# A three-block network at float32 accuracy on one core: the scaling of each head's probabilities moves from GpSimd to VectorE

## The chip, the cores and the metric

The kernel runs on one core of a Trainium2 chip. The metric is the device time of one execution in microseconds (us). The core has five engines that run their own instruction streams and meet at semaphores: TensorE (PE in the profile, with PEld for its weight loads), VectorE (DVE), ScalarE (ACT), GpSimd (POOL) and SyncE (SP), which here issues the weight loads from memory.

## The reference

An input of 256 rows by 1024 features goes through a stack of layers. In short, and cut to what matters here:

```
h = x
h = h + moba_nsa_mixer(rmsnorm(h));  h = h + relu(rmsnorm(h) @ w1)**2 @ w2      # "even" mixer, then an MLP
h = h + fox_mixer(rmsnorm(h));       h = h + relu(rmsnorm(h) @ w1)**2 @ w2      # "fox" mixer, then an MLP
h = rmsnorm(h)
h = h + 0.5 * gate1 * swiglu(n1)                                                # gated MLP
h = h + gate2 * hybrid_mixer(n2)                                                # "dil" mixer
h = h + 0.5 * gate3 * swiglu(n3);  return rmsnorm(h)
# in each mixer, for each head, with 256 queries and 256 keys of 64 features:
s = q @ k.T * scale + bias;  s = where(mask, s, -inf)
p = exp(s - max(s)) / sum(exp(s - max(s)))         # softmax over the keys
o = gate * (p @ v)                                 # gate: a sigmoid per row, only in the NSA branches
```

The even mixer has 24 such heads: 16 NSA heads (8 heads in two branches, "selected" and "window", each with a gate per query row) and 8 MoBA heads without a gate. The fox mixer has 16 heads, the dil mixer 8, all without a gate. A ninth NSA branch over 15 compressed keys is computed beside the heads.

## The kernel before

**Weights.** 512 KB halves of the weights stream through a ring of four units. ScalarE rounds each half (`w_hi`, L737), VectorE computes the rest (`w_lo`, L1141), and TensorE multiplies with three products (high by low, low by high, high by high), which gives float32 accuracy. Each unit counts in `unit_used` when TensorE is done, and SyncE then loads the unit that takes its place.

**Mixers.** A mixer is a list of ticks, a tick being a half or a quarter of a weight unit of a projection. `plan` at the top of the file fixes, before the kernel is built, which heads' scores, turns and products lie in which tick; all engines walk through the same list. In a tick TensorE does, in this order: the scores of a head (`scores`, L1872 and L1873, into one PSUM bank, `BANK_S`), the turning (transposition) of the probabilities of an earlier head (`turn_probs`, L1881), for two heads at a time the products with the values (`products`, L1899), the extras of the mixer, and then its part of the projection (L1662 to L1664).

**One head.** After the scores VectorE adds the bias and finds the row minimum of the negated logits (L1352, `logit` and `low`, once for query rows 128 to 255 with 256 keys, once for query rows 0 to 127 with 128 keys). ScalarE takes the exponential into `prob` (L908), with the row sums in `den`, and counts `probs_ready`. VectorE takes the reciprocals of the two sums (L1371, `wgt`, 128 x 2). GpSimd multiplies `prob` in place by the reciprocal and by the gate (`scale`, L599), a column of 128 x 1 each, or by the constant 1.0 where the head has no gate, and counts `probs_scaled`. TensorE waits for that in `turn_probs`, some two ticks later. There are four `prob` buffers, two `logit` buffers, but only one scores bank: TensorE may write the scores of head i only when VectorE has finished the logits of head i-1:

```
if i >= 1:
    pe.wait_ge(logits_ready, i)
```

**VectorE's tick**, in program order: the logits of the tick's head, the split of a finished projection (`stack`, L1333, two instructions, after the last tick of a unit), the copy of a turned odd head (L1364, `probT`), one half of `w_lo` where one is due, the reciprocals (L1371), the extras, and the split of finished output tiles (L1377). The extras in the even mixer are the steps of the compressed branch (L1549 to L1551, L1561 to L1564, L1569 to L1574). Instructions on an engine start in program order, so what stands behind a long one waits for it. The helper `chain(ins)` makes VectorE wait until `ins` has been completed.

**GpSimd's stream** between the scalings: it sets zeros, issues small loads, and in the fox mixer `mask(c)` adds the causal triangle to the gates of four heads at a time (L607, L608), each of which VectorE waits for before the first logits of those four heads.

Of the kernel before, what the change touches and what calls it, by code (L numbers as in the profile page):

```python
# [22 lines left out]
ALU = mybir.AluOpType  # L23
# [60 lines left out]
EVEN, FOX, DIL = (0, 24), (24, 40), (40, 48)  # L84
# [102 lines left out]
def build(nc, stream, ada, cols, x, c_row, rel_table, rel_pick, dil_bias, pool_mat, b_forget, final_norm, g_final, out):  # L187
    ctx = ExitStack()
    with ctx:
        base = [-(-nc.sbuf_base // 64) * 64]  # L190

        def place(name, shape, dt=F32, at=None):
            size = -(-int(np.prod(shape[1:])) * 4 // 64) * 64
            if at is None:
                at = base[0]
                base[0] += size
            return nc.alloc_sbuf_tensor_at(name, list(shape), dt, offset=at)

        def sem(name):
            return ctx.enter_context(nc.semaphore(name))  # L200
# [50 lines left out]
        prob = place("prob", [P, 4, SW])  # L251
# [21 lines left out]
        den = place("den", [P, CMP_COL + 16])  # L273
        wgt = place("wgt", [P, CMP_COL + 16])
        gates = place("gates", [P, TT, 24])
# [100 lines left out]
        weight_ready = sem("weight_ready")  # L376
        probs_scaled = sem("probs_scaled")
# [46 lines left out]
        heads = []  # L424
# [10 lines left out]
        for hh in range(HEADS):  # L435
# [3 lines left out]

        TILES = {"even": [(4, 0, 0), (5, 0, T), (6, 1, 0), (7, 1, T)] + [(m, m % 2, 0) for m in range(4)],  # L440
                 "fox": [(m, m % 2, 0) for m in range(8)], "dil": [(m, m % 2, 0) for m in range(4)]}
        TILES_BEFORE = {"even": 0, "fox": 8, "dil": 16}

        def out_col(i):
# [141 lines left out]
        def _(pool):  # L586
# [3 lines left out]
                pool.memset(k_lo2[0:HD, tiles, 1, :].bitcast(F32), 0.0).then_inc(zeros_ready, 1)  # L590
                pool.wait_ge(zeros_ready, before + 2)

            def scale(first, last):
                for i in range(first, last):
                    pool.wait_ge(weight_ready, i + 1)
                    for t, lo, hi in ((1, 0, 256), (0, 256, 384)):
                        p_ = prob[:, i % 4, lo:hi]
                        gate = 1.0 if heads[i][5] is None else gates[:, t, heads[i][5]:heads[i][5] + 1]
                        ins = pool.tensor_scalar(p_, p_, wgt[:, 2 * i + t:2 * i + t + 1], gate, ALU.mult, ALU.mult)  # L599
                    ins.then_inc(probs_scaled, 1)  # L600

            def mask(c):

                pool.wait_ge(cum_landed[c], 16)
                four = slice(4 * c, 4 * c + 4)
                tri = pc_("tri", P).unsqueeze(1).to_broadcast([P, 4, P])
                pool.tensor_tensor(cum_early[:, four, :], cum_row[:, four, 0:P], tri, ALU.add).then_inc(masked, 1)  # L607
                pool.tensor_tensor(cum_row[:, four, P:T], cum_row[:, four, P:T], tri, ALU.add).then_inc(masked, 1)  # L608
# [18 lines left out]
            def store_gate(j):  # L627
                pool.wait_ge(gain_ready, j + 1)
                pool.dma_start(bass.AP(gate_dram, j * D, [[KT, P], [1, KT]]), gatec[:, KT * j:KT * j + KT]).then_inc(gate_stored, 16)
# [18 lines left out]
            pool.dma_start(rel_band[:, HEADS:16, :], bass.AP(rel_dram, HEADS * (REL + 1), [[1, P], [REL + 1, HEADS], [1, T]])).then_inc(rel_landed[0], 16)  # L648
            pool.wait_ge(unit_used, FIRST["kskw"])
            pool.dma_start(rel_band[:, 0:HEADS, :], bass.AP(rel_dram, 0, [[1, P], [REL + 1, HEADS], [1, T]])).then_inc(rel_landed[1], 16)  # L650
            scale(*EVEN)

            pool.wait_ge(bank_turned, TURN["mlp0"] + 8)
            zeros(slice(6, 8), 2)
# [10 lines left out]
            def forget_gates(c):  # L665
                if c > 0:
                    pool.wait_ge(unit_used, FIRST["qk_fox"] + c - 1)
                pool.dma_start(cum_row[:, 4 * c:4 * c + 4, :], bass.AP(cum_dram, 4 * c * T, [[0, P], [T, 4], [1, T]])).then_inc(cum_landed[c], 16)
# [4 lines left out]
            mask(1)  # L673
            forget_gates(2)
            forget_gates(3)
            scale(FOX[0], FOX[0] + 2)
            mask(2)
            scale(FOX[0] + 2, FOX[0] + 6)
            mask(3)
            scale(FOX[0] + 6, FOX[1])  # L680

            pool.wait_ge(bank_turned, TURN["mlp1"] + 8)
            pool.wait_ge(unit_used, FIRST["mlp1"] + 3)
# [19 lines left out]
            pool.wait_ge(bank_turned, TURN["gmix"] + 8)  # L703
            gate_rows(1)
            store_gate(2)
            scale(*DIL)

            round_half("gf2")
            pool.wait_ge(bank_turned, TURN["gf2"] + 8)
# [415 lines left out]
        def _(dve):  # L1125
            steps = [0]

            def chain(ins):
                steps[0] += 1
                ins.then_inc(dve_step, 1)  # L1130
                dve.wait_ge(dve_step, steps[0])
# [3 lines left out]
            def rest_half():  # L1135

                if halves[0] < 2 * N_UNITS:
                    u, part = halves[0] // 2, halves[0] % 2
                    dve.wait_ge(hi_ready, halves[0] + 1)
                    part_ = slice(HALF * part, HALF * part + HALF)  # L1140
                    nc.vector.tensor_tensor(w_lo[:, u % RING, part_], raw[:, u % RING, part_], w_hi[:, u % RING, part_].bitcast(F32),  # L1141
                                            ALU.subtract).then_inc(lo_ready, 1)
                    halves[0] += 1
# [181 lines left out]
            def stack(key, halves_=(0, 1)):  # L1325
                bank, keys, tile = STACKS[key]
                for b in halves_:
                    dve.wait_ge(feat_hi, 2 * STACK_NO[key] + b + 1)
                    rows_ = slice(HD * b, HD * b + HD)
                    src = ps[bank][rows_, :].rearrange("p (a b) -> p a b", a=2)  # L1330
                    hi = (k_two if keys else q_two)[rows_, tile:tile + 2, b, :]
                    dst = k_lo2[rows_, tile:tile + 2, b, :] if keys else q_two[HD * (1 - b):HD * (1 - b) + HD, tile:tile + 2, b, :]
                    ins = nc.vector.scalar_tensor_tensor(out=dst, in0=src, scalar=1.0 if keys else -0.125, in1=hi.bitcast(F32),  # L1333
                                                         op0=ALU.mult, op1=ALU.subtract)
                    ins.then_inc(feat_taken, 1)
# [6 lines left out]
            def mixer(kind, ticks, extras):  # L1342
                prev = None
                for tick in ticks:
                    for i in tick.s:
                        bias = heads[i][4]
                        dve.wait_ge(scores_done, i + 1)
                        if i >= 2:
                            dve.wait_ge(probs_ready, i - 1)
                        for t, lo, hi in ((1, 0, 256), (0, 256, 384)):  # L1350
                            kk = 2 * i + t
                            ins = nc.vector.tensor_tensor_reduce(  # L1352
                                logit[:, i % 2, lo:hi], ps[BANK_S][:, lo:hi], bias(t),
                                1.0, 4 * BIG, ALU.add, ALU.min, low[:, kk:kk + 1])
                        ins.then_inc(logits_ready, 1)
                    stacks = prev is not None and prev.part == prev.parts - 1 and (prev.tag, prev.j) in STACKS
                    if stacks:
                        stack((prev.tag, prev.j), (0,))
                    for j in tick.t:
                        if j % 2:  # L1360
                            dve.wait_ge(probsT_done, j + 1)
                            if j >= TURNED:
                                dve.wait_ge(pv_done, (j - TURNED) // 2 + 1)
                            nc.vector.tensor_copy(probT[:, j % TURNED, :], ps[BANK_PT][:, 0:SW]).then_inc(probsT_dve, 1)  # L1364
                    if stacks:
                        stack((prev.tag, prev.j), (1,))
                    if halves[0] < tick.halves:
                        rest_half()
                    for i in tick.s:
                        dve.wait_ge(probs_ready, i + 1)  # L1370
                        nc.vector.reciprocal(wgt[:, 2 * i:2 * i + 2], den[:, 2 * i:2 * i + 2]).then_inc(weight_ready, 1)  # L1371
                    extras(tick)
                    if prev is not None:
                        for n in prev.closed:
                            m, bank, c0 = TILES[kind][n]
                            dve.wait_ge(tile_hi, TILES_BEFORE[kind] + (n | 1 if kind == "even" and n < 4 else n) + 1)
                            nc.vector.tensor_tensor(q_two[:, m, 1, :], ps[bank][:, c0:c0 + T], q_two[:, m, 0, :].bitcast(F32),  # L1377
                                                    ALU.subtract).then_inc(tile_split, 1)
                    prev = tick
# [280 lines left out]
        def _(pe):  # L1660
# [223 lines left out]
            def products(kind, i):  # L1884
# [5 lines left out]
                if i >= NSA:  # L1890
# [3 lines left out]
                    elif n >= 2:  # L1894
                        pe.wait_ge(tile_split, TILES_BEFORE[kind] + n - 1)
                for block, lo, hi in ((0, 0, T), (1, T, SW)):
# [8 lines left out]
            def out_part(kind, j, part, parts=4):  # L1905
# [4 lines left out]
                elif part == 0:  # L1910
                    pe.wait_ge(tile_split, TILES_BEFORE[kind] + 2 * ((j - 2 if kind == "dil" else j) + 1))
                if part == 0 and j == 0:
# [380 lines left out]
```

## Time and profile before

| | |
|---|---|
| median of 3 runs | 1077.68 us (1077.62 to 1077.70) |
| the profiled execution | 1077.94 us, of which the traced span is 1075.8 us |
| busy, share of the span | PE 99%, DVE 74%, ACT 62%, POOL 11% |
| granted TensorE clock | 0.999 of full speed |

How to read it: the span is the time from the first to the last instruction of the trace; the profiled execution took 2.1 us more than its span. A busy share is an average over stages. PE is counted as busy when matmuls overlap one another, so a short hold of TensorE can hide in longer intervals between matmuls.

### The profile page before, as it was taken

Reading aid. Unit: us, or ns where it says so; the run is one execution under the profiler, and the core shown is the slowest. Engines: PE = TensorE matmul, PEld = TensorE weight load, DVE = VectorE, ACT = ScalarE, POOL = GpSimd, SP = SyncE. Lnnn points to the kernel's source line nnn. Section 1 sums busy time; section 2 is a strip of 40 time slices with the busy share of each in tenths; the row PEclk is TensorE's granted clock in tenths of the full one; section 3 lists DMA queues with packets and bytes.
Section 4 is the critical chain, followed back from the end, with each engine's and each line's share of the span. In section 5 each row is a group of like instructions: output and inputs, shape, how many; then the busy total and the mean of one; then the engine's idle time right before and its main releaser. Section 6 shows DMA issues by size and latency. Waiting matters only on the chain.

```text
span 1075.8 us, 16103 instructions
## 1 busy us (share of the span) xinstructions
PE 1065.0 (99%) x6102; PEld 915.4 (85%) x6102; DVE 792.8 (74%) x1384; ACT 669.7 (62%) x1186; POOL 119.1 (11%) x212
## 2 busy tenths in 40 slices
PE   9999999999999999999999999999999999999997
PEld 7998788888888997888888888888878978888885
DVE  7767677787877776787767788987885778566575
ACT  7678677565666776766556765454476767445443
POOL 1033110010100531020000000111000210000000
PEclk9999999999999999999999999999999999999999
DMA  9932359888865633687877568878745445565551
GB/s 360 326 127 86 111 176 341 290 300 301 305 217 170 229 127 111 214 322 264 282 244 272 181 213 296 294 265 319 275 164 187 139 155 181 193 196 195 182 191 59
DMA packets 65533, 238.33 MB, mean 222 GB/s; under 512 B 7429, under 2 KB 8613, under 8 KB 64688
## 3 DMA queue, kind: packets, MB, share of 16 engines
q1 hardware_dynamic: 51696, 188.82, 51.8%
q0 software_dynamic: 13040, 47.85, 11.9%
q8 instruction: 49, 0.80, 0.3%
q10 hardware_dynamic: 720, 0.62, 0.2%
q14 instruction: 28, 0.23, 0.1%
HBM read 236.15 MB, written 1.11 MB: 221 GB/s over the span
## 4 chain that ended last, share of the span: by engine, by line
PE 93%; DVE 4%; ACT 1%; issue 1%; DMA 0%; POOL 0%; DVEq 0%; ACTq 0%
PE bank L1693 23%; PE bank L1662 15%; PE bank L1663 15%; PE bank L1664 15%; PE bank L1697 12%; PE bank L1830 2%; PE bank L1899 1%; PE bank L1881 1%; PE bank L1720 1%; PE bank L1715 1%; PE bank L1723 1%; PE bank L1768 1%; PE bank L1873 1%; PE bank L1872 1%; DVE w_lo L1141 1%
## 5 line engine op out<-in xcount | busy, mean ns | idle before, releaser
L1141 DVE TENSOR_TENSOR w_lo<-raw,w_hi 128x1024 fp32r<-128x1024 f32 x348 | 414.2, 1229 | 68.3 <-ACT w_hi L737 65.8
L737 ACT ACTIVATE w_hi<-raw 128x1024 fp32r<-128x1024 f32 x345 | 348.8, 1052 | 64.4 <-DMA raw<-in_stream 64.1
L1693 PE MATMUL bank<-a_two,w_hi 128*128 128x512 f32 x1088 | 271.9, 392 | 0.0
L1693 PEld LDWEIGHTS bank<-a_two,w_hi 128*128 128x128 f32 x1088 | 198.4, 188 | 37.4
L946 ACT ACTIVATE cross<-bank 128x256 f32<-128x256 f32 x136 | 51.4, 381 | 190.7 <-PE bank L1697 190.5
L1662 PE MATMUL bank<-w_lo,hid_hi 128*128 128x512 f32 x432 | 169.2, 392 | 0.2
L1663 PE MATMUL bank<-w_hi,hid_lo 128*128 128x512 f32 x432 | 168.7, 390 | 0.0
L1664 PE MATMUL bank<-w_hi,hid_hi 128*128 128x512 f32 x432 | 168.1, 389 | 0.0
L1697 PEld LDWEIGHTS bank<-a_two,w_lo 128*128 128x128 f32 x1088 | 148.4, 190 | 10.6
L1697 PE MATMUL bank<-a_two,w_lo 128*128 128x256 f32 x1088 | 151.7, 282 | 0.0
L1385 DVE TENSOR_TENSOR hid_act<-bank,cross 128x256 f32<-128x256 f32 x96 | 39.6, 422 | 86.7 <-ACT cross L946 86.5
L1664 PEld LDWEIGHTS bank<-w_hi,hid_hi 128*128 128x128 f32 x432 | 81.1, 188 | 17.2
L1662 PEld LDWEIGHTS bank<-w_lo,hid_hi 128*128 128x128 f32 x432 | 81.3, 188 | 16.5 <-DVE hid_lo L1392 1.0
L1663 PEld LDWEIGHTS bank<-w_hi,hid_lo 128*128 128x128 f32 x432 | 81.3, 188 | 14.9
L1662 PE MATMUL bank<-a_two,w_hi 128*128 128x256 f32 x320 | 93.5, 292 | 0.0
L1664 PE MATMUL bank<-a_two,w_hi 128*128 128x256 f32 x320 | 90.4, 283 | 0.0
L1663 PE MATMUL bank<-a_two,w_lo 128*128 128x256 f32 x320 | 90.4, 282 | 0.0
L1419 DVE CUSTOM_DVE_ANT_0 ada_raw<-ada_raw,silu_row 128x1024 f32<-128x1024 f32 x72 | 84.8, 1219 | 4.3 <-DMA ada_raw<-in_ada 2.3
L614 POOL DMA_DIRECT2D ada_raw<-in_ada x72 | 38.1, 530 | 322.5 <-DVE modc L1419 322.5
L1662 PEld LDWEIGHTS bank<-a_two,w_hi 128*128 128x128 f32 x320 | 61.1, 191 | 2.4 <-issue 2.1
L1663 PEld LDWEIGHTS bank<-a_two,w_lo 128*128 128x128 f32 x320 | 61.2, 191 | 0.1
L1664 PEld LDWEIGHTS bank<-a_two,w_hi 128*128 128x128 f32 x320 | 61.1, 191 | 0.0
(234 smaller groups left out, 1339.9 us busy)
## 6 DMA issues: line engine op xcount, KB each, us to landing
raw<-in_stream SPq DMA_DIRECT2D x348, 512.0 KB, 5.0
ada_raw<-in_ada POOLq DMA_DIRECT2D x72, 512.0 KB, 5.3
cmpw<-in_stream SPq DMA_DIRECT2D x4, 1024.0 KB, 9.6
rel_band<-rel_scratch POOLq DMA_DIRECT2D x2, 1024.0 KB, 11.2
cum_row<-cum_scratch POOLq DMA_DIRECT2D x4, 512.0 KB, 5.7
gate_row<-gate_scratch POOLq DMA_DIRECT2D x3, 512.0 KB, 6.3
h<-in_x SPq DMA_DIRECT2D x2, 512.0 KB, 4.4
silu_row<-in_c_row POOLq DMA_DIRECT2D x2, 512.0 KB, 6.4
```

Source lines behind the costliest of these rows:

```text
L614: pool.dma_start(ada_raw[:, p % ADA_BUFS, :], ada[p]).then_inc(ada_landed[p % ADA_BUFS], 16)
L737: nc.scalar.activation(w_hi[:, u % RING, part_], raw[:, u % RING, part_], ACT.Copy).then_inc(hi_ready, 1)
L946: nc.scalar.activation(cross[:, slot, nt, :], ps[bank][:, T:2 * T], ACT.Copy).then_inc(done, 1)
L1141: nc.vector.tensor_tensor(w_lo[:, u % RING, part_], raw[:, u % RING, part_], w_hi[:, u % RING, part_].bitcast(F32), ALU.subtract).then_inc ...
L1385: nc.vector.tensor_tensor(to[:, nt * T:(nt + 1) * T], ps[bank][:, 0:T], cross[:, slot, nt, :], ALU.add).then_inc(done, 1)
L1419: nc.vector.tensor_tensor_reduce(part, part, silu_row[:, :], 1.0, 0.0, ALU.mult, ALU.add, modc[:, p:p + 1]).then_inc(ada_done, 1)
L1662: nc.tensor.matmul(dst, l_hi, r_lo, start=start, stop=False)
L1663: nc.tensor.matmul(dst, l_lo, r_hi, start=False, stop=False)
L1664: return nc.tensor.matmul(dst, l_hi, r_hi, start=False, stop=stop)
L1693: nc.tensor.matmul(ps[bank][:, 0:2 * T], wh[:, k, cols_], a_two[:, :, k, :], start=k == 0, stop=False)
L1697: ins = nc.tensor.matmul(ps[bank][:, T:2 * T], wl[:, k, cols_], a_hi[:, k, :], start=False, stop=k == KT - 1)
L1830: ins = nc.tensor.matmul(ps[BANK_A[2 * t + n]][:, 0:w], rows_[:, 2 * j + k, ts], weights[:, k, 512 * n:512 * n + w], start=(j, k, term) == ...
```

## The change

The 96 GpSimd instructions that scale the probabilities (2 for each of 48 heads) are removed, with their function. VectorE issues the same two multiplications itself, in place, behind the reciprocals of the head, and counts `probs_scaled`. Between the reciprocals and the first multiplication VectorE waits for the reciprocals' completion (`chain`). `weight_ready` is no longer counted, since all three mixers are in `SCALED_BY_DVE`. GpSimd's masks of heads 8 to 15 of the fox mixer stand directly behind its loads.

```
+        SCALED_BY_DVE = ("even", "fox", "dil")
...
-            def scale(first, last):
-                for i in range(first, last):
-                    pool.wait_ge(weight_ready, i + 1)
-                    for t, lo, hi in ((1, 0, 256), (0, 256, 384)):
-                        p_ = prob[:, i % 4, lo:hi]
-                        gate = 1.0 if heads[i][5] is None else gates[:, t, heads[i][5]:heads[i][5] + 1]
-                        ins = pool.tensor_scalar(p_, p_, wgt[:, 2 * i + t:2 * i + t + 1], gate, ALU.mult, ALU.mult)
-                    ins.then_inc(probs_scaled, 1)
...
-            scale(*EVEN)
...
-            scale(FOX[0], FOX[0] + 2)
             mask(2)
-            scale(FOX[0] + 2, FOX[0] + 6)
             mask(3)
-            scale(FOX[0] + 6, FOX[1])
...
-            scale(*DIL)
...
                     for i in tick.s:
                         dve.wait_ge(probs_ready, i + 1)
-                        nc.vector.reciprocal(wgt[:, 2 * i:2 * i + 2], den[:, 2 * i:2 * i + 2]).then_inc(weight_ready, 1)
+                        weights_ = nc.vector.reciprocal(wgt[:, 2 * i:2 * i + 2], den[:, 2 * i:2 * i + 2])
+                        if kind not in SCALED_BY_DVE:
+                            weights_.then_inc(weight_ready, 1)
+                            continue
+                        chain(weights_)
+                        for t, lo, hi in ((1, 0, 256), (0, 256, 384)):
+                            p_ = prob[:, i % 4, lo:hi]
+                            gate = 1.0 if heads[i][5] is None else gates[:, t, heads[i][5]:heads[i][5] + 1]
+                            ins = nc.vector.tensor_scalar(p_, p_, wgt[:, 2 * i + t:2 * i + t + 1], gate, ALU.mult, ALU.mult)
+                        ins.then_inc(probs_scaled, 1)
```

On VectorE, in the even mixer, this is the stretch of heads 11 to 13 of the kernel before: the reciprocals of head 11, the logits of head 12, a copy, a weight half, the reciprocals of head 12 and the compressed branch ahead of the logits of head 13.

```order
L1371 RECIPROCAL wgt<-den 128x2
L1352 ISA logit,low<-bank,rel_band 128x256
L1352 ISA low 128x1
L1352 ISA logit,low<-bank,rel_band 128x128
L1352 ISA low 128x1
L1364 COPY probT<-bank 128x384
L1141 TENSOR_TENSOR w_lo<-raw,w_hi 128x1024
L1371 RECIPROCAL wgt<-den 128x2
L1569 TENSOR_REDUCE den<-pc 128x16
```

The same stretch on VectorE with the change (line numbers there are those of the changed file: L1358 is the reciprocal, L1339 the logits, L1366 the new multiplication, L1128 the weight half):

```order
L1358 RECIPROCAL wgt<-den 128x2
L1366 TENSOR_SCALAR prob<-prob,wgt,gates 128x256
L1366 TENSOR_SCALAR prob<-prob,wgt,gates 128x128
L1339 ISA logit,low<-bank,rel_band 128x256
L1339 ISA low 128x1
L1339 ISA logit,low<-bank,rel_band 128x128
L1339 ISA low 128x1
L1351 COPY probT<-bank 128x384
L1128 TENSOR_TENSOR w_lo<-raw,w_hi 128x1024
L1358 RECIPROCAL wgt<-den 128x2
L1366 TENSOR_SCALAR prob<-prob,wgt,gates 128x256
L1366 TENSOR_SCALAR prob<-prob,wgt,gates 128x128
```

Each head's two multiplications now stand between its reciprocals and the logits of the next head.

On GpSimd, in the fox mixer, the scalings of the kernel before stand between the third load (issued twice in a row for heads 8 to 11 and 12 to 15) and the mask of heads 8 to 11:

```order
L668 DMA cum_row<-cum_scratch 128x1024 x2
L599 TENSOR_SCALAR prob<-prob,wgt 128x256
L599 TENSOR_SCALAR prob<-prob,wgt 128x128
L599 TENSOR_SCALAR prob<-prob,wgt 128x256
L599 TENSOR_SCALAR prob<-prob,wgt 128x128
L607 TENSOR_TENSOR cum_early<-cum_row,par 128x512
L608 TENSOR_TENSOR cum_row<-cum_row,par 128x4x128
L599 TENSOR_SCALAR prob<-prob,wgt 128x256
```

The same place on GpSimd with the change (L659 is the load, L599 and L600 the mask):

```order
L659 DMA cum_row<-cum_scratch 128x1024 x2
L599 TENSOR_TENSOR cum_early<-cum_row,par 128x512
L600 TENSOR_TENSOR cum_row<-cum_row,par 128x4x128
L599 TENSOR_TENSOR cum_early<-cum_row,par 128x512
L600 TENSOR_TENSOR cum_row<-cum_row,par 128x4x128
L609 DMA silu_row<-in_c_row 128x1024
```

The two masks follow the loads directly, and GpSimd then waits for the MLP.

## Rows read from the trace of the kernel before

**Rows 1.** The page: busy time of each engine, and the chain's shares.

```profile
PE 1065.0 (99%) x6102; PEld 915.4 (85%) x6102; DVE 792.8 (74%) x1384; ACT 669.7 (62%) x1186; POOL 119.1 (11%) x212
...
PE 93%; DVE 4%; ACT 1%; issue 1%; DMA 0%; POOL 0%; DVEq 0%; ACTq 0%
```

**Rows 2.** The stretch 76 to 92 us: busy time and number of instructions.

```profile
76.00:92.00 16.00, 15.73 (x140) 14.60 (x139) 12.76 (x49) 11.79 (x33) 5.61 (x12) 1.00 0.20 67
```

**Rows 3.** The chain that ended last, in the even mixer: start, us, what.

```profile
78.72 0.17 DVE wgt L1371
```

**Rows 4.** TensorE's timeline: start of the scores of heads 11 to 14.

```profile
80.75 0.28 PE L1872 MATMUL bank<-k_two,q_two 128*128 128x256 f32 x1
...
84.59 0.28 PE L1872 MATMUL bank<-k_two,q_two 128*128 128x256 f32 x1
...
86.78 0.28 PE L1872 MATMUL bank<-k_two,q_two 128*128 128x256 f32 x1
...
90.16 0.35 PE L1872 MATMUL bank<-k_two,q_two 128*128 128x256 f32 x1 [0.27 <-DVE low L1352]
```

**Rows 5.** VectorE's timeline: heads 11 to 14, and head 18.

```profile
81.91 0.16 DVE L1371 RECIPROCAL wgt<-den 128x2 f32<-128x2 f32 x1
...
83.61 0.42 DVE L1352 CUSTOM_DVE_ANT_0 logit<-bank,rel_band 128x256 f32<-128x256 f32 x1
...
85.60 0.17 DVE L1371 RECIPROCAL wgt<-den 128x2 f32<-128x2 f32 x1
85.80 0.42 DVE L1352 CUSTOM_DVE_ANT_0 logit<-bank,rel_band 128x256 f32<-128x256 f32 x1
...
87.96 0.15 DVE L1371 RECIPROCAL wgt<-den 128x2 f32<-128x2 f32 x1
...
89.39 0.41 DVE L1352 CUSTOM_DVE_ANT_0 logit<-bank,rel_band 128x256 f32<-128x256 f32 x1
...
91.07 0.17 DVE L1371 RECIPROCAL wgt<-den 128x2 f32<-128x2 f32 x1 [1.05 <-ACT prob L908]
...
104.16 0.42 DVE L1352 CUSTOM_DVE_ANT_0 logit<-bank,rel_band 128x256 f32<-128x256 f32 x1 [1.93 <-PE bank L1873]
```

**Rows 6.** TensorE's timeline: the scores of head 18.

```profile
103.54 0.28 PE L1872 MATMUL bank<-k_two,q_two 128*128 128x256 f32 x1
```

**Rows 7.** GpSimd's scalings: count, duration min/median/max in ns, starts.

```profile
L599 POOL TENSOR_SCALAR prob<-prob,wgt x64: 364/479/1423, 100.2 to 865.5; 128x256 f32<-128x256 f32 x32, 128x128 f32<-128x128 f32 x32
L599 POOL TENSOR_SCALAR prob<-prob,wgt,gates x32: 436/502/561, 53.1 to 98.0; 128x256 f32<-128x256 f32 x16, 128x128 f32<-128x128 f32 x16
```

**Rows 8.** VectorE's groups by form: busy us, mean ns of one.

```profile
L1189 DVE TENSOR_SCALAR tok<-h,stat 128x512 f32<-128x512 f32 x11 | 5.2, 485 | 0.3
...
L1176 DVE TENSOR_SCALAR stat<-stat 128x1 f32<-128x1 f32 x14 | 3.0, 214 | 4.8 <-ACT tok L753 4.4
...
L1167 DVE TENSOR_SCALAR stat<-stat 128x1 f32<-128x1 f32 x14 | 2.0, 146 | 0.1
...
L1648 DVE SCALAR_TENSOR_TENSOR tok<-h,stat,row 128x256 f32<-128x256 f32 x4 | 1.8, 481 | 0.1
```

**Rows 9.** VectorE's timeline: a scaling of 512 columns and its successor.

```profile
609.25 0.49 DVE L1189 TENSOR_SCALAR tok<-h,fin 128x512 f32<-128x512 f32 x1
609.66 1.22 DVE L1141 TENSOR_TENSOR w_lo<-raw,w_hi 128x1024 fp32r<-128x1024 f32 x1
```

**Rows 10.** TensorE's timeline: scores of heads 11 and 12 of the fox mixer.

```profile
401.39 0.28 PE L1872 MATMUL bank<-k_two,q_two 128*128 128x256 f32 x1
...
403.54 0.36 PE L1872 MATMUL bank<-k_two,q_two 128*128 128x256 f32 x1
```

**Rows 11.** VectorE's timeline: a weight half in the fox mixer.

```profile
358.37 2.07 DVE L1141 TENSOR_TENSOR w_lo<-raw,w_hi 128x1024 fp32r<-128x1024 f32 x1 [0.30 <-ACT w_hi L737]
```

**Rows 12.** The chain in the dil mixer.

```profile
854.00 0.69 DVE q_two L1333
...
854.98 1.88 POOL prob L599 x2
```

## The prediction

> **What bounds the kernel now.** I read the page first, then the busy time by stretch, then the chain that ended last, then the timelines of single engines. TensorE is busy for 99% of the span, and the chain runs through it for 93%, but 4% of it, some 43 us, lie on VectorE [rows 1]. So the question is where TensorE is held by VectorE, and how close VectorE is to holding it elsewhere. In the middle of the even mixer the chain leaves TensorE for more than 11 us: it stands on VectorE at 78.72 with the reciprocals of a head, and comes back with the scores of head 14 at 90.16 [rows 3, 4]. In the 16 us around it VectorE is busy for 12.76 and ScalarE for 11.79 [rows 2]. TensorE shows only one hold there, 0.27 us ahead of those scores [rows 4]. So this stretch is balanced: TensorE and VectorE both run almost without slack, and the link is the single scores bank.
>
> Three intervals describe the link. From the start of the scores to the start of the logits, 0.62 us (103.54 and 104.16, where VectorE had been waiting) [rows 5, 6]. From the start of the logits to the earliest start of the next scores, 0.77 us (89.39 and 90.16) [rows 4, 5]. From the start of the logits to the start of the reciprocals when only the exponential lies between, 1.68 us (89.39 and 91.07) [rows 5]; I use 1.70. I call these starts S, L and R.
>
> **What is removed.** 96 GpSimd instructions with medians of 0.48 and 0.50 us [rows 7]. Nothing but the turns of TensorE waits for them, two ticks later, and POOL has no measurable share of the chain [rows 1]. One place shows: in the dil mixer a pair took 1.88 us and the chain goes through it [rows 12]. I value what comes back there at 0.2 us.
>
> **What is added.** Two VectorE multiplications for each head. The trace has no such instruction of 256 or 128 columns, but it has the same operation at other sizes: 146 ns with one column and two constants, 214 ns with one column and one operand per partition, 485 ns with 512 columns [rows 8]. A per-partition operand thus adds 68 ns and a column (485 - 214) / 512 = 0.53 ns. That gives 350 and 282 ns without a gate, 418 and 350 ns with one. An instruction's successor starts some 0.075 us before its end (609.25 to 609.66 for 0.485) [rows 9], but not across a wait for completion: head 11's reciprocals take 0.17 and the logits start 0.20 behind them [rows 5]. So in place of one interval of 0.20 there are 0.20, then 0.34, then 0.38: s = 0.71 us with a gate and, the same way, 0.58 without. Over 16 gated and 32 other heads this is 29.9 us more on VectorE, and the sum depends on how much of it TensorE's ticks absorb.
>
> The Trainium skill (VectorE: DVE Perf Modes, the section on the TRN2 errata) gives 58 cycles plus columns over the mode's factor for such an instruction; at 0.96 GHz and factor 2 that is an estimate of 0.33 us for 512 columns, where this trace has 0.485. By the page, s would be 0.44 us or less and the sum below about 4 us. The measured row decides here.
>
> **The even mixer, worked.** Each head obeys: S is the tick's place in TensorE's stream plus the delay p so far, or the previous L + 0.77, whichever is later, and in the second case p grows by the difference. L is S + 0.62, or the time when VectorE is free. R is L + 1.70, or L + 0.65 plus what stands between (1.60 for a copy and a weight half, 1.40 for a split projection, about 1.1 for a weight half alone). VectorE is then free at R + 0.10 + s plus its extras. With s = 0 this recurrence gives back the trace to about 0.1 us, with a hold of 0.4 where the trace has 0.27, and 0.1 more at the end. With s = 0.71 it reaches head 10 with p = 1.12 (grown at heads 2, 3 and 6, where a weight half or a split stands in the tick) and L = 81.59. From there, with the starts of before from [rows 4, 5]:
>
> Head 10 has R = 81.59 + 0.65 + 1.60 = 83.84; with 0.81 and the compressed branch's 1.62 (81.91 to 83.61 less the usual interval) head 11 has L = 86.27. Its scores would start at 80.75 + 1.12 = 81.87 but wait for 81.59 + 0.77 = 82.36: p = 1.61. Head 12's would start at 84.59 + 1.61 = 86.20 and wait for 87.04: p = 2.45. Head 11 has R = 88.32, so head 12 has L = 89.13; head 13's scores go from 89.23 to 89.90: p = 3.12. Head 12 has R = 91.38, and with 0.81 and 1.33 of the branch (87.96 to 89.39) head 13 has L = 93.52; head 14's scores, unheld at 89.89 + 3.12 = 93.01, wait for 94.29: p = 4.40. Behind it ticks with products and longer parts absorb the additions (before head 18 VectorE had waited 1.93 us [rows 5]), until heads 22 and 23 add 0.7 and 0.2: p = 5.26. The same recurrence without the additions has 0.52, so the term is **+4.7 us**.
>
> **The fox mixer.** Its ticks hold half a weight unit, not a quarter, and by the recurrence the additions of 0.58 are absorbed up to head 11. From there the ticks are the quarters of the output projection, 2.15 us (401.39 to 403.54) [rows 10]: the logits of heads 12 and 13 come 0.7 and 1.5 later, and two holds of 0.5 and 0.9 follow. The term is +1.3, less what s = 0 gives in the same recurrence (0.2): +1.2 us.
>
> **The dil mixer.** The same pattern at heads 4 to 6, and the split that ends at 854.69, for which TensorE waits already [rows 12], now begins 0.7 later, since the logits in front of it are late. Holds of 0.7, 0.1 and 0.5, less 0.2 for the pair that took 1.88: +1.2 us.
>
> Sum: 4.7 + 1.2 + 1.2 = 7.1 us. The profiled execution took 1077.94 us (span 1075.8); with 7.1 that is 1085.0. The median of the runs is 0.26 lower, so I forecast 1085.0 for the median, rounded up by that much. TensorE has hardly any wait behind the mixers in which a delay could be given back, so it stays to the end.
>
> **What hides the rest.** Of 29.9 us some 23 cost nothing, because VectorE stood waiting for scores (1.93 before head 18) or for the exponential. If the exponential moves with the late logits, that second cover is gone; the recurrence has this in it.
>
> **The masks.** GpSimd's masks of heads 8 to 15 now run back to back near 369 us. A weight half on VectorE, which takes 1.22 elsewhere [rows 9], took 2.07 beside an earlier mask [rows 11], 0.85 more. At worst two of VectorE's instructions are held so, in the long ticks that absorb the additions. I take nothing, with an upper end of 1.5 us. The Trainium skill (SBUF — State Buffer, section Who interferes with whom) has a rule for this: a GpSimd instruction and a VectorE instruction in a two-port mode or with two SBUF inputs exclude each other for their whole length. The 2.07 agrees with it, as does the pair of 1.88.
>
> **Bounds.** For s from below: the shortest form of the operation, 146 ns, and nothing for the wait for completion, would be near 0.3 for both; nearer to the 512-column row is 0.45, at which the recurrence gives 2.4, 0.8 and 0.4, so 3.6 us in all. From above: at the rate of the 256-column row that reads two tiles, 481 ns [rows 8], the first multiplication costs 0.13 more and the second 0.07, and with another 0.05 for the second operand s is 0.95, which gives 7.6, 1.6 and 2.0, with the masks 12 us. The operation itself is nearest to the 485 ns row, so I take 0.71.
>
> **Rivals.** (a) *Dearer multiplications*, s near 0.9, with or without the masks: +9.5 to +12, about 1088.5. For it: in-place operands and short tiles that no row shows. Against: three rows of the same operation lie on one line. 0.15. (b) *Cheaper, better hidden*, s near 0.5 or a TensorE stream with more give than the recurrence allows, as its 0.4 for 0.27 hints: +2.5 to +4.5, about 1081.5. 0.17. (c) *Absorbed: not slower.* The scores of the next head are late only if VectorE's backlog exceeds the slack of the tick; if TensorE's short matmuls were themselves running behind their weight loads, a hold of up to 0.7 at each score would be made up in the same tick, and the seven holds would vanish. The dil turn then comes 0.2 earlier: 1077.5. It decides if TensorE can make up more than 0.7 us per tick. Against: TensorE is busy for 15.73 of the 16 us [rows 2] and has no idle time to give. 0.08. (d) *The masks as a new wait*: they take VectorE in ticks without slack, 1 to 2 us more, 1086.5, inside my range; it counts with the forecast.
>
> **The numbers.** The forecast, +5 to +9 us, has 0.60, (a) 0.15, (b) 0.17, (c) 0.08. The range 1081.0 to 1089.5 takes in both bounds of s save the very ends. A measurement of this kernel tells about 0.2%, 2.2 us, from no change. (c) and the lowest part of (b) give same 0.08; faster, which no mechanism here gives, 0.03; slower 0.89.
>
> **What would show it.** In the profile after: the new VectorE group at 0.42 and 0.35 us with a gate, 0.35 and 0.28 without; TensorE's scores (L1872 before) waiting for VectorE's logits at heads 11 to 14 with a total near 3.5 us, and a chain with several us more on VectorE between 50 and 120 us; the even mixer longer by 4.7, the fox and dil mixers by about 1.2 each; the MLPs unchanged. Wrong would be the whole if the scores of head 14 start before 92, or if the multiplications differ by more than 0.1 us from these durations.

## The result and the profile after

The changed kernel takes 1084.63 us (median of 6 runs, 1084.08 to 1085.26), the kernel before 1077.64 (1077.59 to 1077.70): 1.0064 times as long, 95% interval [1.0053, 1.0075], 7.0 us slower. The profiled execution took 1084.26 us, its span is 1082.5.

The page, to be read against [rows 1]:

```profile
span 1082.5 us, 16103 instructions
...
PE 1067.5 (99%) x6102; PEld 915.1 (85%) x6102; DVE 819.7 (76%) x1480; ACT 670.1 (62%) x1186; POOL 70.4 (7%) x116
...
PE 89%; DVE 7%; ACT 2%; issue 1%; DMA 0%; POOL 0%; DVEq 0%; ACTq 0%; POOLq 0%
```

VectorE is busy for 26.9 us more, with 96 instructions more, GpSimd for 48.7 us less. Of the chain VectorE has 7% in place of 4%, some 30 us more, and TensorE 89% in place of 93%. That is more than the 7.0 us by which the kernel is longer: the chain also turns to VectorE in stretches through which it ran on TensorE before.

The new groups of VectorE by form (count, then busy us and mean ns), against the estimates from [rows 8]:

```profile
L1366 DVE TENSOR_SCALAR prob<-prob,wgt 128x256 f32<-128x256 f32 x32 | 12.0, 374 | 1.1
...
L1366 DVE TENSOR_SCALAR prob<-prob,wgt 128x128 f32<-128x128 f32 x32 | 9.8, 307 | 0.0
...
L1366 DVE TENSOR_SCALAR prob<-prob,wgt,gates 128x256 f32<-128x256 f32 x16 | 6.6, 412 | 0.6
L1366 DVE TENSOR_SCALAR prob<-prob,wgt,gates 128x128 f32<-128x128 f32 x16 | 5.5, 342 | 0.0
```

412 and 342 ns stand against the estimated 418 and 350. Without a gate the means are above the estimated 350 and 282, because of one pair beside GpSimd's masks; the shortest of the 128-column ones took 279, and the medians are 353 and 281.

What TensorE's matmuls waited for (us in total, times, longest us):

```profile
PE bank L1868 <- DVE low L1339: 4.3, 9, 1.0
...
PE bank L1868 <- DVE q_two L1320: 0.2, 1, 0.2
```

The scores (L1868 here) waited nine times for VectorE's logits; before it was one wait of 0.27 us [rows 4]. TensorE's timeline at heads 11 to 14 of the even mixer (start, us, and in brackets the idle time ahead):

```profile
81.96 0.36 PE L1868 MATMUL bank<-k_two,q_two 128*128 128x256 f32 x1 [0.30 <-DVE low L1339]
...
86.53 0.36 PE L1868 MATMUL bank<-k_two,q_two 128*128 128x256 f32 x1 [0.51 <-DVE low L1339]
...
89.43 0.36 PE L1868 MATMUL bank<-k_two,q_two 128*128 128x256 f32 x1 [0.48 <-DVE low L1339]
...
93.62 0.36 PE L1868 MATMUL bank<-k_two,q_two 128*128 128x256 f32 x1 [1.01 <-DVE low L1339]
```

Against [rows 4] these starts are later by 1.21, 1.94, 2.65 and 3.46 us. Head 0's is 0.40 earlier (49.99 against 50.39), which has nothing to do with the scaling: no head has been scaled by then. So the scaling holds TensorE back by 1.61, 2.34, 3.05 and 3.86; the recurrence had 1.61, 2.45, 3.12 and 4.40, the last less 0.27 for the hold that was there before. (The idle times in brackets, 2.3 us in all, are less than the 2.7 us by which the delay grows at these four heads, since a part of each hold hides in longer intervals between matmuls.)

This reading, the start of a head's scores less the start of the same head's in the kernel before, is the measure of all that follows. The table gives by how much it grew from the first to the last head of each mixer, in us (from the timelines of each run's trace):

```
                              even    fox     dil    median of runs   before beside it
changed kernel                4.6     2.0     0.3       1084.63          1077.64
e1 VectorE: even alone        4.6      0       0        1082.11          1077.70
e2 VectorE: fox alone          0      2.1      0        1079.55          1077.70
e3 VectorE: dil alone          0       0      0.3       1077.79          1077.70
e4 masks held back            4.6     1.2     0.3       1083.52          1077.70
e5 scaled twice              13.8     5.5     2.2       1100.37          1077.83
e6 behind next logits         2.6     1.9     0.2       1082.73          1077.83
e7 e6 + masks held back       2.6     1.2     0.2       1081.85          1077.83
e8 e7, behind the split too   2.0     1.35    0.8       1081.96          1077.71
e9 128 columns only           2.25    0.45   -0.3       1079.77          1077.71
```

The last column is the kernel before, run again beside each group of experiments. Each version has one trace.

### The profile page after: what moved, and what is told of

Read it like the earlier page. It is cut to its first block, busy times and chain, and to the rows that moved or that the text cites. A ratio compares the mean times of both kernels' runs of the same rounds, so it can differ in the third digit from the quotient of the medians.

```text
span 1082.5 us, 16103 instructions
## 1 busy us (share of the span) xinstructions
PE 1067.5 (99%) x6102; PEld 915.1 (85%) x6102; DVE 819.7 (76%) x1480; ACT 670.1 (62%) x1186; POOL 70.4 (7%) x116
## 4 chain that ended last, share of the span: by engine, by line
PE 89%; DVE 7%; ACT 2%; issue 1%; DMA 0%; POOL 0%; DVEq 0%; ACTq 0%; POOLq 0%
PE bank L1689 23%; PE bank L1658 14%; PE bank L1659 14%; PE bank L1660 14%; PE bank L1693 12%; PE bank L1826 2%; PE bank L1895 1%; DVE w_lo L1128 1%; PE bank L1716 1%; PE bank L1711 1%; PE bank L1719 1%; PE bank L1877 1%; PE bank L1764 1%; DVE logit L1339 1%; PE bank L1868 1%
## 5 line engine op out<-in xcount | busy, mean ns | idle before, releaser
L1128 DVE TENSOR_TENSOR w_lo<-raw,w_hi 128x1024 fp32r<-128x1024 f32 x348 | 414.1, 1229 | 65.3 <-ACT w_hi L724 62.5
L895 ACT ACTIVATE prob<-logit,low 128x256 f32<-128x256 f32 x96 | 42.9, 447 | 36.5 <-DVE low L1339 36.2
```

The source lines that it names most:

```text
L895: ins = nc.scalar.activation(prob[:, i % 4, lo:hi], logit[:, i % 2, lo:hi], ACT.Exp, scale=-1.0, bias=low[:, kk:kk + 1], accum_out=den[:, ...
```

## The experiments

**Each mixer alone (e1, e2, e3).** The scaling by GpSimd is put back for the mixers that `SCALED_BY_DVE` doesn't name:

```
-        SCALED_BY_DVE = ("even", "fox", "dil")
+        SCALED_BY_DVE = ("even",)          # e1;  ("fox",) in e2;  ("dil",) in e3
```

> VectorE scales in the even mixer alone; GpSimd scales in the fox and dil mixers as before. Theory (the delay is the sum of the holds at the scores bank, mixer by mixer): TensorE ends the even mixer 4.2 us later in the trace of the changed kernel (head 23's scores at 121.25 against 117.07), and nothing gives it back, so +4.2 us, 1081.9; by the recurrence of the prediction +4.7, 1082.4. Rival (a general cost of 29.9 us more work on VectorE, shared out by heads): 15.4 of the 29.9 us of scaling are in the even mixer by number and length, so 16*0.71 + 8*0.58 = 16.0 of 29.9, +3.7 us.

> VectorE scales in the fox mixer alone. Theory: the fox mixer adds 2.0 us in the trace of the changed kernel, 0.94 at head 3, beside the masks, and 1.0 at heads 13 to 15, so 1079.6. In this kernel the masks of heads 8 to 15 run back to back too. The prediction had +1.2, 1078.9. Rival (shared out by heads): 9.3 of 29.9 us, +2.2 us; the two are not told apart by this run alone.

> VectorE scales in the dil mixer alone. Theory: +0.3 us, 1078.0, as the spacing of the scores in the trace of the changed kernel says. The prediction had +1.2, 1078.9. Rival (shared out by heads): 4.6 of 29.9 us, +1.1 us.

Measured against the kernel before: e1 1.0041 [1.0027, 1.0056], +4.4 us; e2 1.0019 [1.0009, 1.0028], +1.85 us; e3 1.0001 [0.9992, 1.0010], +0.1 us, which is no difference. The three add up to 6.4 of the 7.0 us; in the traces they grow by what they grow in the changed kernel, mixer by mixer. The delay is a sum of separate holds. A cost shared out by heads would have had 3.7 us in the even mixer, 2.2 in the fox and 1.1 in the dil mixer. The intervals of e1 and e2 hold these values too, and 1.1 us lies at the edge of the interval of e3; against it speaks the dil mixer's 0.3 in the traces, and what decides is e5, e6 and e9 below.

**The masks (e4).**

```
+            pool.wait_ge(probs_scaled, FOX[0] + 2)
             mask(2)
+            pool.wait_ge(probs_scaled, FOX[0] + 6)
             mask(3)
```

The two masks wait for the scaling of heads 1 and 5, behind which they stood before.

> The changed kernel, but GpSimd waits for the scaling of heads 1 and 5 of the fox mixer before it makes the third and the fourth mask, so that these stand where they stood before. Theory (the hold of 0.78 us at head 3 comes from the masks of heads 8 to 15 running back to back at 369 to 374 us and blocking VectorE's scaling pair of 2.04 us): that pair falls to 0.55 us and the kernel is 0.9 us faster than the changed one, 1083.7. Rival (the hold comes from the additional work alone, and the masks would only hold something else): within 0.2 us of the changed kernel, 1084.6.

Measured: 1083.52 us, 1.0055 [1.0038, 1.0072] against before; over before it has 5.8 us where the changed kernel has 7.0. The intervals of the two overlap, though no run of e4 (1083.37 to 1083.69) is as long as the shortest of the changed kernel (1084.08); the traces decide. VectorE's timeline in the changed kernel:

```profile
369.97 1.34 DVE L1128 TENSOR_TENSOR w_lo<-raw,w_hi 128x1024 fp32r<-128x1024 f32 x1 [0.26 <-ACT w_hi L724]
...
371.43 2.04 DVE L1366 TENSOR_SCALAR prob<-prob,wgt 128x256 f32<-128x256 f32 x2
373.49 0.42 DVE L1339 CUSTOM_DVE_ANT_0 logit<-bank,cum_row 128x256 f32<-128x256 f32 x1
...
376.09 0.42 DVE L1339 CUSTOM_DVE_ANT_0 logit<-bank,cum_row 128x256 f32<-128x256 f32 x1
```

and GpSimd's at the same time:

```profile
370.20 2.07 POOL L600 TENSOR_TENSOR cum_row<-cum_row,par 128x512 f32<-128x512 f32 x1
372.24 1.14 POOL L599 TENSOR_TENSOR cum_early<-cum_row,par 128x512 f32<-128x512 f32 x1
```

The pair takes 2.04 us in place of 0.55, and the mask addition that began at 370.20 takes 2.07 in place of 1.08. Read with their ends, these are two meetings in a row. The addition had begun beside the weight half (369.97 to 371.31), and from the end of that half it lasted another 0.96 us. The pair's first multiplication, begun at 371.43, took 1.00 us and ended 0.15 behind that addition, at 372.42; the second took 1.12, beside the next addition (372.24 to 373.38). In each case the one that began later ended behind the other, by its own usual length or less. The scores of head 3, at 374.28, then waited 0.78 us for the logits of head 2, and the fox mixer fell behind by 0.94 there. With the masks held back this hold is gone and the fox mixer grows by 1.2 us, not 2.0. A pair still meets a mask in e4 (1.19 us at 374.37), but the delay grows by no more than 0.2 us behind it. The Trainium skill (SBUF — State Buffer, section Who interferes with whom) says that a GpSimd instruction and a VectorE instruction in a two-port mode exclude each other for their whole length; the pair, which gets on only when the addition ahead of it ends, agrees.

**Twice the scaling (e5).** The additional results go into a buffer that is free by then, and nothing reads them (shortened, with `...` for the indices of `wgt`):

```
+                            nc.vector.tensor_scalar(logit[:, i % 2, lo:hi], p_, wgt[...], gate, ALU.mult, ALU.mult)
                             ins = nc.vector.tensor_scalar(p_, p_, wgt[...], gate, ALU.mult, ALU.mult)
```

> The changed kernel, with each scaling done twice on VectorE: an additional multiplication of the same form writes into the logits buffer, which is free by then. Adds 0.61 us per gated and 0.49 us per other head, 25.4 us of work on VectorE. Theory (slack once used up, every further us goes to TensorE; recurrence with 1.32 and 1.07 us per head): the even mixer +15.0 over the kernel before, fox +3.0, dil +2.7, so 14 us over the changed kernel, 1098.5. Rival (a fixed share, 7.0 us for 29.9 us of work, holds on): +6 us over the changed kernel, 1090.6.

Measured: 1100.37 us, 1.0209 [1.0192, 1.0226], +22.5 us over before and 15.7 over the changed kernel: some 25 us of work cost 15.7, where the first 30 had cost 7.0. The fixed share is refuted. The even mixer has 13.8 where the recurrence had 15.0, dil 2.2 for 2.7, but fox 5.5 for 3.0. There the masks hold VectorE (0.99 and 1.18 us for multiplications of 0.35 at 381.84 and 382.75), TensorE stands for 1.84 us, and then this is seen, in TensorE's timeline and in the busy time by stretch (the column before the last two is the granted clock):

```profile
382.91 0.28 PE L1660 MATMUL bank<-a_two,w_lo 128*128 128x256 f32 x1
383.03 0.28 PE L1661 MATMUL bank<-a_two,w_hi 128*128 128x256 f32 x1
385.15 0.36 PE L1869 MATMUL bank<-k_two,q_two 128*128 128x256 f32 x1 [1.84 <-DVE low L1339]
...
386.89 0.41 PE L1661 MATMUL bank<-a_two,w_hi 128*128 128x256 f32 x1
387.11 0.41 PE L1659 MATMUL bank<-a_two,w_hi 128*128 128x256 f32 x1
```

```profile
383.00:386.00 3.00, 1.16 (x8) 0.99 (x7) 2.97 (x8) 0.96 (x5) 0.78 (x1) 0.90 0.52 162
386.00:389.00 3.00, 3.00 (x17) 3.00 (x16) 2.90 (x12) 2.95 (x9) 0.00 (x0) 0.53 0.49 191
389.00:392.00 3.00, 3.00 (x28) 3.00 (x28) 2.90 (x8) 1.52 (x3) 0.00 (x0) 1.00 0.02 5
```

Behind the idle 1.84 us the matmuls follow at 0.21 us in place of 0.12, at a clock of 0.53, nearly all of it at the 1.2 GHz level, until about 389. The tick took 5.22 us (385.15 to 390.37) instead of 3.63: 1.6 us more, behind a hold of 1.84. Not every such hold does this: three others of e5, of 1.56, 1.59 and 1.55 us in the even mixer (scores of heads 11, 14 and 22), left the clock at 1.00, so these traces don't give the idle time at which it falls. No hold in the mixers of the changed kernel was longer than 1.01 us, and its clock stood at 1.00 there.

**The same work off the path (e6, e7).** VectorE scales head i only after the logits of head i+1:

```
                         ins.then_inc(logits_ready, 1)
+                    settle()                    # here in short: wait for the reciprocals, the two multiplications, probs_scaled
                     stacks = prev is not None and prev.part == prev.parts - 1 ...
```

> The changed kernel, but VectorE scales head i only behind the logits of head i+1, in the time in which it would otherwise wait for the exponential; the completion wait behind the reciprocals is then met already. Same instructions, same work. Theory (what costs is the time between the reciprocals and the next logits, since the scores bank waits for these): holds shrink, by the recurrence to 2.8 - 0.5 in the even mixer, 1.0 in fox and 0.4 in dil, so +3.7 us over the kernel before, 1081.3. Rival (VectorE's total work in the mixer decides): no change against the changed kernel, 1084.6. Second rival: the turns wait for the later scaling, and it is slower than the changed one, 1086 or more.

> The kernel of e6_late with the masks held back as in e4_masks_late. Theory: the masks cost 0.9 us here too if the additional work meets them in the same tick, so 0.9 faster than e6_late, 1080.4; but if the later place of the scaling takes VectorE out of the masks' way, no difference. Rival (work decides): 0.9 us faster than the changed kernel only, 1083.7.

Measured: e6 1.0045 [1.0030, 1.0060], +4.9 us (expected +3.7); e7 1.0036 [1.0023, 1.0050], +4.0 us, 0.9 less than e6 as expected. The even mixer falls from 4.6 to 2.6 with the same instructions, so their place matters and not only their number: the rival that total work decides, which wanted no change, is refuted. But 2.0 us of the even mixer remain at heads 12 to 14 and 22, and the fox mixer gains nothing. What TensorE waited for in e7:

```profile
PE bank L1890 <- DVE probT L1368: 0.9, 3, 0.4
PE bank L1881 <- DVE low L1355: 0.9, 3, 0.3
PE bank L1881 <- DVE q_two L1323: 0.7, 3, 0.3
```

The wait for the logits is down from 4.3 us to 0.9, but two others have grown in its place: the split of the projection (`q_two`, 0.2 us in the changed kernel) and the copy of turned probabilities (`probT`, none listed for the turns there) now stand behind the scaling.

**Behind those too (e8).** `settle()` stands after the split and the copy, ahead of the weight half; masks held back as in e4.

> The kernel of e7_late_masks_late, but the scaling of the previous head stands behind the split of the projection and the copy of turned probabilities, ahead of the weight half. Theory (in e7 the scaling delays, besides the logits, the split and the copy, and TensorE waits for these at heads 4 and 12 of the even mixer, and at heads 12 to 15 of the fox mixer): the holds on q_two and probT go, the holds on the logits stay; even +2.1, fox +0.6, dil +0.2 over the kernel before, 1080.5, that is 1.3 faster than e7. Rival (what remains is VectorE's total work): the same as e7, 1081.8. Second rival (the turn comes too late now): slower than e7.

Measured: 1.0039 [1.0024, 1.0054], +4.25 us, the same as e7 and not 1.3 faster. In the even mixer it went as expected (2.0), in the fox and dil mixers the second rival came true:

```profile
407.35 0.55 PE L1890 MATMUL bank<-par,prob 128*128 128x128 f32 x3 [1.22 <-DVE prob L1342]
```

The turn waits 1.22 us for the scaling, and another one 1.21 in the dil mixer: the multiplications now stand behind the second half of the split, at 406.75, while TensorE comes to the turn directly behind the scores of 405.48. Each of the three places tried in VectorE's tick had TensorE waiting for something.

**Only 128 columns (e9).** GpSimd scales the 256 columns, VectorE the 128, counted in a semaphore of their own, `early_scaled`, which the turn waits for as well (VectorE's part, shortened):

```
+                        weights_.then_inc(weight_ready, 1)
+                        dve.wait_ge(weight_ready, i + 1)
+                        nc.vector.tensor_scalar(prob[:, i % 4, 256:384], ..., wgt[:, 2 * i:2 * i + 1], gate, ...).then_inc(early_scaled, 1)
```

> VectorE scales the 128 columns of each head only, directly behind its reciprocals; GpSimd scales the 256 columns as before. Adds 0.38 us per gated and 0.31 us per other head on the path from the reciprocals to the next logits, 16 us in all. Theory (holds grow faster than the addition; recurrence with 0.38 and 0.31): even 2.4 - 0.5 = +1.9, fox 0.9 - 0.2 = +0.7, dil +0.2, together +2.7 over the kernel before, 1080.4. Rival (a fixed share of the work, 7.0 for 29.9 us): 16 us give +3.7, 1081.4. Second rival (the completion wait and the order cost, not the length): near the changed kernel, 1083 or more.

Measured: 1.0019 [1.0009, 1.0028], +2.1 us; expected +2.7, fixed share +3.7, which is outside the interval. The second rival, that the completion wait and the order cost and not the length, wanted 1083 or more and is refuted as well: both are there in e9. The even mixer grows by 2.25 (+1.9 expected), fox by 0.45 (+0.7), and dil shrinks by 0.3: GpSimd's pair that took 1.88 us [rows 12] no longer keeps the turn of head 3 waiting (that turn began 0.37 us behind the matmul ahead of it, and begins 0.11 behind it in e9). With e9, the changed kernel and e5, 0.38, 0.71 and 1.32 us per gated head (0.31, 0.58 and 1.07 without a gate) cost 2.25, 4.6 and 13.8 us in the even mixer. By these prices its 24 heads add 8.6, 16.0 and 29.7 us on VectorE, and of each further us 0.26 reach TensorE at first, then 0.32, and at last 0.67: cheap while slack is there, and dearer the less is left.

No version is faster than the kernel before. For the scaling GpSimd is the better of the two engines tried, since its queue is the one for which hardly anybody waits. Whether ScalarE, busy for 62%, could do it was not tried.

## Why the prediction was right

**The bound.** Right: TensorE and VectorE were balanced in the even mixer, and the single scores bank ties them. From head 11 on the holds came at the heads that the recurrence named, with the delay within 0.1 us of it up to head 13 and 0.3 at head 14. Ahead of that only the sum was right: the recurrence had 1.12 us from heads 2, 3 and 6, the trace has 1.15 from heads 3, 4 and 5 (0.58, 0.47 and 0.09), of which the one at head 4 is a wait for the split and not for the logits.

**The price of a head.** Right for the instructions, 412 and 342 ns with a gate for 418 and 350, and medians of 353 and 281 without for 350 and 282. The time from a head's reciprocals to the next logits, 0.20 us where they follow directly, was 0.79 behind heads 0 to 2 and 0.90 behind heads 3 and 11, so 0.59 to 0.70 more for s = 0.71; without a gate it was 0.66 or 0.77 for 0.19, so 0.47 to 0.58 more for 0.58. The s of the sum is the upper end of both. The Trainium skill's row (VectorE: DVE Perf Modes, the section on the TRN2 errata) had given an estimate of 0.33 us for 512 columns, and with it below about 4 us in all; [rows 8] has 0.485, and the kernel lost 7.0.

**The even mixer.** Forecast +4.7, measured 4.6 in the trace and 4.4 by e1. That is close partly by luck, as the places of the early holds and the upper end for s show.

**The fox mixer.** Forecast +1.2, measured 2.0. The step that failed is "I take nothing" for the masks: they cost 0.8 us in the traces (2.0 less the 1.2 of e4) and 1.1 to 1.2 by the medians, mostly as one hold of 0.78 at head 3. The holds at the output ticks, 0.4 and 0.5 at heads 13 and 14, came where expected and smaller than the forecast 0.5 and 0.9.

**The dil mixer.** The term was mis-sized: forecast +1.2, measured 0.3, and no difference by e3. The statement that the split "begins 0.7 later" was wrong. The scores of head 3 started at 857.83 and its logits at 858.72, 0.89 us behind, so only 0.27 later than the usual 0.62, and the split moved with them. Head 2's logits had been 0.57 later against its scores than before. Of that, 0.18 went between them and the reciprocals (1.70 us apart, 1.88 before, when they were not bound by the weight half alone), and 0.12 more behind those, where the addition took the 0.61 us that VectorE had waited for the scores of head 3. Instead of the forecast 0.7, 0.1 and 0.5 at heads 4 to 6, less 0.2 for GpSimd's pair, the delay grew by 0.15 and 0.18 and then fell by 0.09. The two errors, 0.8 too little for fox and 0.9 too much for dil, nearly cancel; the forecast of 1085.0 owes its closeness to the result to that luck as well. (Two roundings are in it as well: the addends for dil give 1.1 and not 1.2, and the median as worked out is 1084.8.)

**The rivals.** Absorption (c) is refuted in the even mixer: TensorE made up nothing of a hold in the same tick, and the delays stand unchanged through ticks with slack (3.86 at heads 14 to 21). Dearer (a) multiplications fail by the measured durations. So do cheaper ones (b); its other half, better hidden ones, is true of the dil mixer alone, and 7.0 us is outside its +2.5 to +4.5. The masks (d) happened, at about 1 us, the lower end of the 1 to 2 of the forecast.

**The start.** Head 0 is 0.40 us earlier than before without a scaling ahead of it. Of this, 0.15 is there from about 10 us on. The other 0.25 is a hold in the trace of the kernel before. There ScalarE waited 0.86 us for the weight half of 37.89 to land, VectorE was some 0.8 us late from there on, and its split ended late for head 0's scores, which began 0.38 us behind the matmul ahead of them, against 0.12 in the changed kernel. VectorE's split in the kernel before and in the changed one:

```profile
49.56 1.41 DVE L1333 SCALAR_TENSOR_TENSOR q_two<-bank,q_two 64x512 fp32r<-64x512 f32 x2
...
48.78 1.41 DVE L1320 SCALAR_TENSOR_TENSOR q_two<-bank,q_two 64x512 fp32r<-64x512 f32 x2
```

The other ten traces don't have this hold (e6 a small part of it), e2 and e3 included, whose even mixer GpSimd scales as before. So it belongs to that execution, and the measure, which starts at head 0, leaves out all but 0.07 us of it. The other 0.15 scatters between the traces (in e3 it is 0.14 the other way by head 0), and its cause was not looked for.

## What to carry to other kernels

When an engine's work moves to another, ask first who waits for the new engine next, not how much time it has free: VectorE was 26% idle, and 30 us of cheap work still cost 7.0. Walk along the shortest loop between the two engines (here scores, logits, exponential, reciprocals, next logits), one tick after another, with the durations of the trace; slack is used up tick by tick, and each further us costs more than the one before it (0.26, 0.32 and 0.67 in the even mixer). If work must go on a full engine, put it in the loop's idle part, and then look again at what stands behind it in the queue, since each place tried here had somebody waiting. And hold the instructions of two engines that met badly before against the new order of both queues: the term taken as nothing, the masks, was the one that grew.

## What the hardware showed unexpectedly

A single idle time of 1.84 us on TensorE (e5) was followed by about 3.5 us at 1.2 GHz, which cost another 1.6 us, while three idle times of 1.55 to 1.59 us in the same run, and those up to 1.2 us in the mixers of the others, left the clock at 1.00. And a pair of VectorE multiplications of 0.55 us took 2.04 us beside GpSimd's additions: each waited for the addition beside it. One of these additions had itself taken 2.07 us in place of 1.08, because it had begun during a weight half of VectorE. Who began first went through at about its usual length, and the other lost.
